# Output projection of a two-layer hybrid decoder: 7 block products for 8 in three of the eight units of its later column parts

## What is computed

```python
for l in range(DEPTH):                                   # 2
    h = _rmsnorm(x, attn_norm[l])
    proj = jnp.einsum('bsd,de->bse', h, w_in[l])
    ...
    mixed = jnp.concatenate([o_diff, o_gla, o_mla], axis=-1)      # 256 x 2048
    x = x + jnp.einsum('bse,ed->bsd', mixed, w_out[l])            # w_out: 2048 x 2048
    h2 = _rmsnorm(x, ffn_norm[l])
    ff = jax.nn.silu(jnp.einsum('bsd,df->bsf', h2, w_gate[l])) * jnp.einsum('bsd,df->bsf', h2, w_up[l])
    x = x + jnp.einsum('bsf,fd->bsd', ff, w_down[l])
return _rmsnorm(x, final_norm)
```

## Time and profile before

| | |
|---|---|
| Three runs | 2184.55, 2185.74, 2187.57 us; median 2185.74 |
| The profiled execution | 2186.89 us, its span 2185.1 us |
| Mean granted clock of TensorE | 0.998 of full speed |
| TensorE matmul busy | 2163.6 us (99%) |
| VectorE busy | 1715.3 us (78%) |
| ScalarE busy | 1083.2 us (50%) |
| Moved by DMA | 402.77 MB, 184 GB/s |

### The profile page before, as it was taken

One profiled execution on the slowest core, in us unless ns is written; L12 is line 12 of the kernel. 1 busy time (PEld: TensorE's weight loads), 2 busy tenths in 40 slices (PEclk: granted clock), 3 DMA queues, 4 the chain that ended last, 5 costly groups with the idle time before them and its releaser, 6 DMA issues.

```text
span 2185.1 us, 27181 instructions
## 1 busy us (share of the span) xinstructions
PE 2163.6 (99%) x10826; PEld 1843.1 (84%) x10826; DVE 1715.3 (78%) x1934; ACT 1083.2 (50%) x1142; POOL 24.0 (1%) x24
## 2 busy tenths in 40 slices
PE   8999999999999999999999999999999999999998
PEld 7899988888888888888888999888878888888886
DVE  5576774788898888889755867747888898888886
ACT  5454543554554545545443645435545454445443
POOL 0000000000000000000000000000000000000000
PEclk9999999999999999999999999999999999999999
DMA  7544455555655565565555434555555655665664
GB/s 249 181 133 131 140 178 185 181 193 194 204 198 192 193 207 194 194 207 194 192 180 166 146 111 161 174 177 192 193 192 196 206 193 193 199 204 192 201 202 154
DMA packets 221103, 402.77 MB, mean 184 GB/s; under 512 B 13376, under 2 KB 53600, under 8 KB 220896
## 3 DMA queue, kind: packets, MB, share of 16 engines
q1 hardware_dynamic: 220304, 400.90, 55.8%
q10 hardware_dynamic: 720, 0.78, 0.1%
HBM read 399.54 MB, written 2.10 MB: 184 GB/s over the span
## 4 chain that ended last, share of the span: by engine, by line
PE 95%; DMA 2%; DVE 1%; ACT 1%; issue 1%; SPq 0%; POOLq 0%; POOL 0%; ACTq 0%; DVEq 0%
PE bank L1014 19%; PE bank L1016 19%; PE bank L1015 19%; PE bank L693 10%; PE bank L695 10%; PE bank L694 10%; PE bank L653 2%; DMA stage<-in_w_in 1%; PE bank L818 1%; DMA stage<-in_w_down 1%; ACT w_hi L1177 1%; PE bank L759 0%; PE bank L882 0%; DVE w_lo L1532 0%; PE bank L870 0%
## 5 line engine op out<-in xcount | busy, mean ns | idle before, releaser
L1532 DVE TENSOR_TENSOR w_lo<-stage,w_hi 128x2048 fp32r<-128x2048 f32 (+4 forms) x319 | 679.4, 2132 | 272.6 <-ACT w_hi L1177 272.2
L1177 ACT ACTIVATE w_hi<-stage 128x2048 fp32r<-128x2048 f32 (+4 forms) x319 | 569.3, 1787 | 393.5 <-DMA stage<-in_w_down 192.1
L693 PE MATMUL bank<-w_hi,xt_hi 128*128 128x512 f32 (+4 forms) x1048 | 376.8, 360 | 6.6 <-DVE xt_lo L1593 4.2
L695 PE MATMUL bank<-w_hi,xt_lo 128*128 128x512 f32 (+4 forms) x1048 | 369.5, 353 | 0.0
L694 PE MATMUL bank<-w_lo,xt_hi 128*128 128x512 f32 (+4 forms) x1048 | 369.3, 352 | 0.0
L1014 PE MATMUL bank<-w_hi,xt_hi 128*128 128x512 f32 x812 | 316.4, 390 | 0.0
L1016 PE MATMUL bank<-w_hi,xt_lo 128*128 128x512 f32 x812 | 315.9, 389 | 0.0
L1015 PE MATMUL bank<-w_lo,xt_hi 128*128 128x512 f32 x812 | 315.9, 389 | 0.0
L1014 PE MATMUL bank<-w_hi,f_hi 128*128 128x512 f32 x696 | 273.2, 392 | 2.4 <-DVE kept L2016 1.5
L1016 PE MATMUL bank<-w_hi,f_lo 128*128 128x512 f32 x696 | 271.0, 389 | 0.0
L1015 PE MATMUL bank<-w_lo,f_hi 128*128 128x512 f32 x696 | 271.0, 389 | 0.0
(11 more groups left out here) (258 smaller groups left out, 2819.2 us busy)
## 6 DMA issues: line engine op xcount, KB each, us to landing
stage<-in_w_gate SPq DMA_DIRECT2D x176, 512.0 KB, 3.8
stage<-in_w_up SPq DMA_DIRECT2D x176, 512.0 KB, 4.7
stage<-in_w_down SPq DMA_DIRECT2D x174, 512.0 KB, 4.6
stage<-in_w_in SPq DMA_DIRECT2D x96, 384.0 KB, 3.7
stage<-in_w_out SPq DMA_DIRECT2D x64, 512.0 KB, 4.4
stage<-in_w_in SPq DMA_DIRECT2D x54, 512.0 KB, 4.7
stage<-in_w_in SPq DMA_DIRECT2D x16, 320.0 KB, 3.4
stage<-in_w_q_b SPq DMA_DIRECT2D x12, 384.0 KB, 3.8
```

The source lines that it names most:

```text
L693: pe.matmul(acc, a, wh[:, i, :], start=first and i == 0, stop=False)
L695: mm = pe.matmul(acc, b, wh[:, i, :], start=False, stop=last and i == len(kts) - 1)
L1177: act.activation(w_hi[s][:, 0:kts * cols], stage[s][:, 0:kts * cols], ACT.Copy).then_inc(hi_made[s], 1)
L1532: vec.tensor_tensor(w_lo[s][:, 0:kts * cols], stage[s][:, 0:kts * cols], w_hi[s][:, 0:kts * cols].bitcast(F32), ALU.subtract).then_inc(lo_ ...
```

## The change

In P2, P3 and P5 the eight block products are made as seven. For that the second pair of column parts is arranged anew: each of the units P0 to P7 now takes two channel tiles for both column parts 2 and 3 (before, four tiles for one). Channel tiles 0 to 2 are paired with 12 to 14 in the set units (`OUT_SETS`); the plain ones take the other ten, two at a time (`OUT_TILES`). So each unit writes banks 0 to 3, set units also banks 4 to 7, and column parts 2 and 3 are both completed by P7 (part 2 in its middle, `out_half`). P0 works by token: its first half needs banks 0 and 1, its second half banks 2 and 3. VectorE makes the token sums of the mixers' outputs in the step of `U_OUT + 5` (`mix_sums`), ScalarE rounds them in the same step, and VectorE makes their low parts in the step of `U_OUT + 7` (`token_rests`). After P5 ScalarE and VectorE combine banks 4 to 7 (`combine_out`) and VectorE adds the result to the residual. `sums` and `sums_hi` get three more buffers each, and `x_whole` another place. The feed-forward stage keeps its work.

```diff
-ACT_LINKS, VEC_LINKS = 9, 68
+ACT_LINKS, VEC_LINKS = 9, 72
...
+OUT_SETS, OUT_PAIRS = (2, 3, 5), (0, 1, 4, 6, 7)
+OUT_TILES = (4, 5), (6, 7), (8, 9), (10, 11), (3, 15)
+U_PAIR = U_OUT + 8
...
+                for i in range(8):
+                    n = U_PAIR + i
+                    s = n % 4
+                    sp.wait_ge(used[s], quad(n) + 1)
+                    view = stage[s][:, :].rearrange("p (b n) -> p b n", b=4)
+                    for part in range(2):
+                        src = w_out[layer, :, (2 + part) * NCH:(3 + part) * NCH]
+                        first, second = (OUT_SETS.index(i),) * 2 if in_set(n) else OUT_TILES[OUT_PAIRS.index(i)]
+                        if in_set(n):
+                            second += 12
+                        src = src.rearrange("(k p) n -> p k n", p=P)[:, first:second + 1:second - first, :]
+                        sp.dma_start(view[:, 2 * part:2 * part + 2, :], src).then_inc(full[s], 16)
...
+                    if first:
+                        need(xs_made, 2, 1)
+                        for r in range(4):
+                            b = norm_bank(layer, "norm2", r)
+                            pe.wait_ge(bank_free[b], ROUND[layer, ("norm2", r)][b] + 1)
+                    product(7, mixed_x[0], summed[1], first, last)
+                    product(5, mixed_x[2], summed[0], first, last)
+                    product(0, mixed_token(0, q), raw[0], False, False)
+                    product(1, mixed_x[3], raw[2], False, False)
+                    product(2, mixed_token(1, q), summed[2], False, False)
+                    product(4, mixed_token(0, 12 + q), raw[1], first, last)
+                    product(6, mixed_x[1], raw[3], first, last).then_inc(used[s], 1)
...
+                    if m == 0:
+                        order = [(part, i, t) for t in range(NT) for part in range(2) for i in range(2)]
+                        need(x_added, X_ADDS, ADDS + NT)
+                    for part, i, t in order:
+                        if m == 0 and (part, i, t) == (0, 0, 1):
+                            need(x_added, X_ADDS, ADDS + 2 * NT)
...
+                need(out_added, 4, 4)
                 norm_turn("norm2", range(KT // 4))
...
+                    if (1 if layer == 0 else 0) <= n < U_FF - LEAD + 1:
+                        prepare(n + LEAD)
+                    if n == U_OUT + 5:
+                        need(xs_raw, 2, 1)
+                        act.activation(xs_hi[:, :, :, :], xs[:, :, :, :], ACT.Copy).then_inc(xs_hi_made, 1)
+                    if n == U_PAIR + OUT_SETS[-1]:
+                        complete(n)
+                        act.activation(out_sums[0][:, :], bank[4][:, :], ACT.Copy).then_inc(out_kept, 1)
...
+                    link(vec.tensor_tensor(x_whole[:, 0:4, :], xt_hi[:, 0:4, :].bitcast(F32), xt_lo[:, 0:4, :].bitcast(F32),
+                                           ALU.add))
+                    link(vec.tensor_tensor(x_whole[:, 4:8, :], xt_hi[:, 12:16, :].bitcast(F32),
+                                           xt_lo[:, 12:16, :].bitcast(F32), ALU.add))
+                    sums_of_tokens()
...
+                    if n == U_OUT + 7:
+                        token_rests(1)
+                    if U_OUT + 6 <= n < U_PAIR:
+                        add_to_resid(n % 2, n % 2, n)
+                    if n == U_PAIR + OUT_SETS[-1] + 1:
+                        combine_out()
+                    if n == U_FF - 1:
+                        add_pair()
...
+                    if n == U_OUT + 5:
+                        mix_sums()
```

More of the change, by code:

```diff
@@ L961, in _, with blocks @@
                         hook(n)
[L963 to L972, removed]
+                def blocks(x, n=4):
+                    return x[:, :].rearrange("p (b n) -> p b n", b=n)
@@ new lines, in out_pair @@
+                def out_pair(n, m):
+                    s = n % 4
+                    pe.wait_ge(lo_made[s], made(layer * QUADS + n // 4, n))
+                    last = m == len(OUT_PAIRS) - 1
+                    order = [(part, i, t) for part in range(2) for i in range(2) for t in range(NT)]
+                    if m == 0:
[4 more added lines that the diff above has]
+                            need(x_added, X_ADDS, ADDS + 2 * NT)
+                        b = 2 * part + i
+                        mm = product(2 * t + part, mixed_token(t, OUT_TILES[m][i]),
+                                     (blocks(w_hi[s])[:, b, :], blocks(w_lo[s])[:, b, :]), m + i == 0, last and i == 1)
+                        if last and (part, i, t) == (0, 1, 1):
+                            mm.then_inc(out_half, 1)
+                    mm.then_inc(used[s], 1)
@@ L973, in _ @@
+                for i in range(8):
+                    if i in OUT_SETS:
+                        out_set(U_PAIR + i, OUT_SETS.index(i))
+                    else:
+                        out_pair(U_PAIR + i, OUT_PAIRS.index(i))
+                    hook(U_PAIR + i)
+                need(out_added, 4, 4)
                 norm_turn("norm2", range(KT // 4))
@@ new lines, in add_pair @@
+                def add_pair():
+                    need(out_added, 4, 4)
+                    for c in (2, 3):
+                        if c == 2:
+                            need(out_half, 1, 1)
+                        else:
+                            complete(U_FF - 1)
+                        for t in range(NT):
+                            cols = resid[:, t, c * NCH:(c + 1) * NCH]
+                            vec.tensor_tensor(cols, bank[2 * t + c - 2][:, :], cols, ALU.add).then_inc(x_added, 1)
@@ L1994, in gate_up @@
                         if i == 6:
[L1995 to L1998 removed]
+                            token_rests(2)
                         if i == 7:
```

186 lines of the change are left out of this document (112 added, 74 removed).

## The result

The changed kernel takes 2194.03 us (median of 8 runs, 2191.65 to 2195.53) beside 2185.23 us for the kernel before (8 runs, 2184.27 to 2187.57): a ratio of 1.0035 (95% interval 1.0026 to 1.0044), slower by 0.3 to 0.4%. The forecast was 2194.6. Its profiled execution took 2193.56 us, with a span of 2191.8.

A forecast was written before the change was run, and what follows sets the result against it. TensorE, busy for 2163.6 of 2185.1 us, was taken as the bound. Per layer -2.06 + 4.3 + 1.1 + 0.6 + 0.5 = +4.4, twice that +8.9, gave 2194.6 us from a median of 2185.74; range 2190.0 to 2199.5.

The forecast's parts named there:

- the sign: Whole kernel: slower, by 0.4%; slower than a measurement can tell from no change was given 0.88 or so.
- the mechanism: In P0's middle TensorE needs column part 1 at 343.2, but VectorE's adds, delayed by queues, end only at 347.3.
- The products: In P2, P3 and P5: 21 matmuls for 24, nine fewer per layer at 0.229 us, -2.06 us per layer.
- The wait in the middle of P0: TensorE waits there for VectorE's adds of column part 1: +4.3 us per layer, bounds 3.8 and 4.8.
- the hand-over to TensorE: From VectorE's adds to TensorE in P0: 0.15 us, an estimate between 0.03 and 0.26.
- The order of causes: Ahead of P0's middle: token sums, ScalarE's xs_hi, then P1's w_hi, VectorE's w_lo and xs_lo, adds until 347.3.
- P3's wait: Ahead of P3 TensorE waits for VectorE's weight sums until 361.6: +1.1 us per layer, bounds 0 and 2.
- the clock: In P0 and P1 TensorE's clock falls after the wait of 4.3 us: +0.5 us per layer, bounds 0 and 1.6.
- Rival (c): Whole kernel: no fall of the clock, the rest as forecast, 2193.6 us; chance 0.24.
- Norm2: Behind P7, the late combination delays column parts 2 and 3: +0.6 us per layer, bounds 0 and 1.5.
- The stretch: P0's start to norm2's first transpose: 47.3 us or a bit more, for 44.0; 42.0 would show it wrong.
- time won elsewhere: If P0's wait is there but the total isn't, the stretch behind norm2 must show the gain; no size given.

The follow-up runs named there:

- e1: Changed kernel without token and weight sums, keeping the 21 matmuls and the combination (doesn't compute the layer): 2181.65 us, 0.9976 of the kernel before.
- e4: Changed kernel with ScalarE rounding P1's weights ahead of xs_hi: 2186.93 us, 1.0002 of the kernel before.
- e9: The kernel before, unchanged, run and profiled again: 2186.40 us, ratio 1.0005.
- e2: Changed kernel's new arrangement only, eight products in all units and none of the added work: 2185.03 us, 0.9993 of the kernel before.
- e5: Changed kernel with both reorderings, ScalarE's of e4 and VectorE's of e3: 2187.27 us, 1.0004 of the kernel before.
- e11: As e6, with sets in P3, P4, P5 and the combination ahead of the first feed-forward unit's preparation: 2182.14 us, 0.9982 of the kernel before.
- e3: Changed kernel with VectorE adding column part 1 ahead of xs_lo: 2194.64 us, 1.0035 of the kernel before.
- e6: As e5, with token sums for three tiles, not four: 2184.56 us, 0.9993 of the kernel before.
- e10: The changed kernel, unchanged, run and profiled again: 2193.78 us, 1.0042 of the kernel before.
- e8: As e5, with only two set units, P2 and P4, and token sums for two tiles: 2182.52 us, 0.9984 of the kernel before.

## Why the prediction was right

The time (2194.03 for 2194.6), the sign and the mechanism were right; that the total came so near is in part luck, as told below. By its own steps, for the two layers of the first profile:

- **The products**, -2.06 us per layer: e1 shows them alone, with 2.0.
- **The wait in the middle of P0**, +4.3: 4.60 and 4.35 by the starts of the matmuls (4.46 and 4.22 as a wait). The adds ended 7.30 us after P0's start (346.07) for 6.86 forecast, and the hand-over to TensorE took 0.05 us for 0.15. (Its upper bound, 0.26 from 384.37, isn't in the rows named: the last matmul's record ends at 384.59 and VectorE starts at 384.63.) The order of causes was right as well: e4 removes ScalarE's step and the adds come 2.9 us earlier.
- **P3's wait and the clock** together, +1.1 + 0.5 = 1.6: the size failed here. The second half of P0 took 2.25 and 1.64 us more, of which 0.12 to 0.15 come without a fall too (e4); 1.6 had been taken from the earlier trace rows, of which 1.1 were to vanish in P3's wait. P3 didn't wait at all. The two cover each other, as the prediction had it, but the clock was the longer of the two. VectorE was done with P3's weights at 360.02 and TensorE came at 361.50. The Trainium skill (TensorE: Matmul & The Clock Gate, "HAM oscillation") has it that idle gaps put the array back to half rate; the two traces of the changed kernel agree, at each of their four waits of over 4 us. Rival (c), no fall, is out by the trace; by the time alone, 2193.6 for 2194.03, it would have looked as good as the forecast.
- **Norm2**, +0.6: +0.24 and +0.37. TensorE was later than forecast, so the combination came relatively earlier; that this is why is argued, no run shows it alone.
- **The stretch** from P0 to the first transpose was given as 47.3 us or a bit more; it is 48.9 and 48.1, for the same reason.

The local sum is therefore +9.6 us (+10.0 in the second profile of the changed kernel), where 8.9 were forecast and the medians differ by 8.8. The prediction said that time won elsewhere must then show behind norm2. It does, by 0.9 us in the first profile of the changed kernel and 1.6 in the second (the next section's load). No term of the forecast has this gain, and it offsets the 0.7 us by which the local sum was too low: the luck in the total.

## What was not expected of the hardware

**A late load that isn't there after the change.** Before, TensorE waits once in the feed-forward stage of the second layer; this is its timeline:

```profile
1621.60 0.50 PE L1014 MATMUL bank<-w_hi,f_hi 128*128 128x512 f32 x1 [1.47 <-DVE kept L2016]
```

VectorE's combination there stands behind a w_lo whose weights landed late. ScalarE's timeline, before and then after:

```profile
1609.61 1.92 ACT L1177 ACTIVATE w_hi<-stage 128x2048 fp32r<-128x2048 f32 x1 [2.62 <-DMA stage<-in_w_down]
1616.70 1.92 ACT L1177 ACTIVATE w_hi<-stage 128x2048 fp32r<-128x2048 f32 x1 [5.17 <-DMA stage<-in_w_down]
1619.99 1.91 ACT L1177 ACTIVATE w_hi<-stage 128x2048 fp32r<-128x2048 f32 x1 [0.89 <-DMA stage<-in_w_down]
```

```profile
1617.25 1.92 ACT L1250 ACTIVATE w_hi<-stage 128x2048 fp32r<-128x2048 f32 x1 [2.89 <-DMA stage<-in_w_down]
1622.78 1.92 ACT L1250 ACTIVATE w_hi<-stage 128x2048 fp32r<-128x2048 f32 x1 [3.62 <-DMA stage<-in_w_down]
1627.97 1.92 ACT L1250 ACTIVATE w_hi<-stage 128x2048 fp32r<-128x2048 f32 x1 [2.79 <-DMA stage<-in_w_down]
```

The distances are 7.09 and 3.29 us before, 5.53 and 5.19 after: the middle unit came some 1.5 us late, though SP issued its loads at the same distances in both (1604.52, 1609.96 and 1614.72 before; 1612.11, 1617.55 and 1622.31 after). One of them took 6.3 us to land (6.2 in e9, 6.1 in e2); at this place of the ten other profiles, all of kernels with 12 or 18 matmuls less, none took over 5.5. Elsewhere loads of over 6 us stand in every profile (6.2 in the changed kernel at 339.38), so what is particular is the place. The wait of 1.3 to 1.5 us is in the same three profiles (before, e9, e2) and in no other. In the ten others the time from the second layer's first feed-forward matmul to the end is 0.8 to 1.6 us shorter, 1.2 in the mean. Why is open: the loads there are the same, and no kernel shifted them alone. With these 1.2 us taken off for the ten, the local times of all kernels but e5 agree with the measured ratios within their intervals (changed: 9.6 - 1.2 = +8.4; e1: -3.2 - 1.2 = -4.4; e4: +1.2; e11: -3.8).

**The clock falls after shorter waits than the one known before.** In full work it held after waits of 1.29 to 1.60 us (e3, e4, e6) and after 1.93 and 1.96 us (e3, second layer), and fell after 1.97 and 1.99 us (e5), 2.24 us (e3, first layer) and 4.2 to 4.5 us (changed, e10). Waits of practically one length, 1.96 and 1.97 us, came out both ways, so near 2 us these rows don't tell what decides. A fall cost 1.64 to 2.25 us in the first profile of the changed kernel, so a wait of 4.5 us costs up to half as much again.

## What to carry to other kernels

A wait that is removed by moving one step in a lagging engine's queue comes back at the next place that this engine feeds, unless the step fills idle time of some engine: e3 moved work within VectorE's full stretch and won nothing that the whole time shows, e4 and e11 filled idle time of ScalarE and VectorE and won 3.2 to 4.0 us per layer and 0.9 us in one layer locally. Work for a nearly idle engine is to be placed by the gaps between its due times, not by its mean load, and fewer savings without a wait (e8) can be worth as much as more of them with waits. Effects of 1 or 2 us are read from the same stretch in two kernels, since whole spans scatter as much and may contain a gain or loss far from the change.
